# Trunk of a hybrid streaming encoder: memory tokens weighted ahead of the query scaling, two gate groups swapped, finer waits

## What is computed

```python
xn = rmsnorm(x, norm1_w)                     # 384 x 1024
proj = xn @ w_in                             # q,k,v | a,b | dn_gate | sc_b,sc_c,sc_h | mq | 3 gates of 1024
q,k,v = split(silu(causal_conv4(qkv)))       # width-4 causal convolution, 12 column groups of 128
q = l2norm(q) * 128**-0.5 ; k = l2norm(k)
o, state = gated_delta(q, k, v, g, beta)     # 64-frame blocks; sample sequences from a carried state
y_dn  = rmsnorm_head(o) * dn_norm_w * silu(dn_gate)        # 512 wide
y_sc  = sc_b * causal_conv3(sc_c * sc_h)                   # 256 wide
y_mem = attend(mq, rmsnorm(mem) @ w_mem_kv)                # 256 wide
merged = sig(g_dn) * (y_dn @ w_br[:512]) + sig(g_sc) * (y_sc @ w_br[512:768]) + sig(g_mem) * (y_mem @ w_br[768:])
h = x + merged @ w_o
y = rmsnorm(h + moe(rmsnorm(h)))             # 32 experts, top 4, 1024 x 1024 x 3 weights each
```

## Time and profile before

| what | value |
|---|---|
| median of the runs | 1447.47 us |
| the profiled execution's own time | 1438.7 us |
| its span, first to last instruction | 1436.8 us |
| PE busy | 1380.6 us (96%) |
| DVE busy | 404.1 us (28%) |
| ACT busy | 232.0 us (16%) |
| chain that ended last | PE 80%, DMA 14%, DVE 3%, ACT 2% |
| mean granted TensorE clock | 0.992 of full |

### The profile page before, as it was taken

How to read it: one execution, slowest core, us unless ns; L and a number is a source line. 1 busy time by engine, 2 the same in 40 slices (tenths; PEclk the granted TensorE clock), 3 DMA queues, 4 the chain that set the end, 5 groups by cost and what they waited for, 6 DMA issues and landing times.

```text
span 1436.8 us, 16371 instructions
## 1 busy us (share of the span) xinstructions
PE 1380.6 (96%) x7269; PEld 672.1 (47%) x7269; DVE 404.1 (28%) x751; ACT 232.0 (16%) x448; POOL 0.2 (0%) x4
## 2 busy tenths in 40 slices
PE   6999999989999899999999999999999999999996
PEld 4546677645554634434434344344343443434432
DVE  3565254261112431221221221212212122121223
ACT  3334231220001111111101111111011111111112
POOL 0000000000000000000000000000000000000000
PEclk9999999999999999999999999999999999999998
DMA  9343331012535589999999999999999999999993
GB/s 339 119 136 118 117 68 61 1 27 92 190 129 234 226 354 429 431 430 430 430 434 428 434 428 432 431 431 432 429 432 430 432 430 430 430 432 430 430 427 148
DMA packets 54072, 455.70 MB, mean 317 GB/s; under 512 B 12532, under 2 KB 21913, under 8 KB 39792
## 3 DMA queue, kind: packets, MB, share of 16 engines
q1 hardware_dynamic: 54000, 454.63, 76.5%
HBM read 449.98 MB, written 4.64 MB: 316 GB/s over the span
## 4 chain that ended last, share of the span: by engine, by line
PE 80%; DMA 14%; DVE 3%; ACT 2%; issue 1%; SPq 0%; DVEq 0%; ACTq 0%
PE ps L1075 38%; DMA sb_ring<-in_w_up_dram 13%; PE ps L752 8%; PE ps L561 7%; PE ps L1112 6%; PE ps L537 4%; PE ps L1051 3%; PE ps L968 3%; PE ps L766 3%; PE ps L601 1%; DVE sb_dg L1634 1%; DMA sb_ring<-in_w_br_dram 1%; PE ps L1012 1%; PE ps L847 1%; DMA sb_cst<-in_consts_dram 0%
## 5 line engine op out<-in xcount | busy, mean ns | idle before, releaser
L1075 PE MATMUL ps<-sb_ring,sb_xg 128*64 128x512 f32 x2048 | 455.6, 597 | 15.8 <-DMA sb_ring<-in_w_up_dram 11.9
L1075 PEld LDWEIGHTS ps<-sb_ring,sb_xg 128*64 128x64 f32 x2048 | 141.8, 137 | 282.9 <-issue 257.4
L1075 PE MATMUL ps<-sb_ring,sb_hidT 128*64 128x512 f32 x1024 | 226.1, 594 | 0.1
L1075 PEld LDWEIGHTS ps<-sb_ring,sb_hidT 128*64 128x64 f32 x1024 | 72.4, 137 | 139.9 <-issue 139.1
L1980 DVE TENSOR_TENSOR sb_hg<-ps,sb_biases 128x512 f32<-128x512 f32 x32 | 22.1, 691 | 404.1 <-PE ps L537 404.1
L752 PE MATMUL ps<-sb_xn,sb_ring 128*128 128x384 f32 x384 | 134.3, 495 | 0.0
L561 PE MATMUL ps<-sb_xn,sb_ring 128*128 128x384 f32 x384 | 126.3, 487 | 1.4 <-DVE sb_xn L1584 1.4
L2004 DVE TENSOR_TENSOR sb_h<-sb_h,ps 128x512 f32<-128x512 f32 x96 | 61.5, 683 | 133.8 <-PE ps L1112 124.0
L561 PEld LDWEIGHTS ps<-sb_xn,sb_ring 128*128 128x128 f32 x384 | 72.2, 190 | 50.8 <-DVE sb_xn L1584 1.8
L752 PEld LDWEIGHTS ps<-sb_xn,sb_ring 128*128 128x128 f32 x384 | 71.3, 191 | 48.6 <-issue 4.3
L1051 PEld LDWEIGHTS ps<-sb_onehot,sb_xn 128*128 128x128 f32 x720 | 81.5, 192 | 12.2 <-issue 12.2
(11 more groups left out here) (305 smaller groups left out, 945.3 us busy)
## 6 DMA issues: line engine op xcount, KB each, us to landing
sb_ring<-in_w_down_dram SPq DMA_DIRECT2D x28, 4096.0 KB, 26.5
sb_ring<-in_w_up_dram SPq DMA_DIRECT2D x27, 4096.0 KB, 29.3
sb_ring<-in_w_gate_dram SPq DMA_DIRECT2D x27, 4096.0 KB, 31.3
sb_ring<-in_w_in_dram SPq DMA_DIRECT2D x12, 2048.0 KB, 9.9
sb_ring<-in_w_gate_dram SPq DMA_DIRECT2D x10, 2048.0 KB, 10.9
sb_ring<-in_w_up_dram SPq DMA_DIRECT2D x10, 2048.0 KB, 14.4
sb_ring<-in_w_down_dram SPq DMA_DIRECT2D x8, 2048.0 KB, 12.6
sb_ring<-in_w_br_dram SPq DMA_DIRECT2D x2, 2048.0 KB, 8.3
```

Of the source, the lines that this page charges most:

```text
L1075: last = mm(o, x(k), columns(kind, w, i, j), start=(k == 0), stop=(k == KT8 - 1))
```

## The change

Four places are touched. The memory tokens' weighting and the last three convolutions stand ahead of the query scaling on VectorE, and TensorE's first memory product waits for one weighted tile and not for both. The sample output goes to words of its own (`o_tok`, in region r1), so that its copy out of PSUM no longer waits for the second output norm; that wait stands behind the transposes now. `output_norm(2, 4)` stands behind the last `mask` and ahead of the merges of that place. `group_unit` puts the gate columns of groups 16 and 17 ahead of both their branch products. The one wait for all 24 merges in front of w_o becomes a wait per block `mg[:, j]` inside the first 8 products.

```diff
--- before.py
+++ after.py
@@ -226,6 +226,7 @@
 
         nwk_s, qd_s = (r1[:, 1024 * k:1024 * k + 1024].rearrange("p (h s n) -> p h s n", h=HEADS, s=NSEQ) for k in range(2))
         oS, osq = t4(wk, 0), t4(wk, 1)
+        o_tok = t4(r1, 6)
         umask = [wk[:, 1024 + 512 * k:1536 + 512 * k].rearrange("p (s v) -> p s v", s=4) for k in range(2)]
 
         mg_at = nc.alloc_sbuf_tensor_at("sb_mg", [P, KT8 * TOK], F32, offset=slab_at + 4 * at["sp"])
@@ -251,6 +252,17 @@
 
         def group_start(k):
             return 10 * k if k <= SIDE else 10 * SIDE + 12 * (k - SIDE)
+
+        def group_unit(u):
+
+            k = next(k for k in range(GROUPS) if u < group_start(k + 1))
+            step = u - group_start(k)
+            if k not in (SIDE, SIDE + 1):
+                return k, step
+            step += 12 * (k - SIDE)
+            if step < 16:
+                return SIDE + step // 8, step % 8
+            return SIDE + (step - 16) // 4, 8 + step % 4
 
         def fill_bank(m):
             return 1 + m % 3
@@ -609,7 +621,7 @@
                     last = mm(bank(0)[32 * r:32 * r + 32, 0:TOK], wab[:, 4 * k + r, :], xnT[:, 4 * k + r, :], start=(k == 0), stop=(k == 1))
             last.then_inc(S["abp"], 1)
 
-            pe.wait_ge(S["xT"], 5)
+            pe.wait_ge(S["xT"], 4)
             weights_in(3)
             memory_columns(0)
             bank_free(PJ_WAB)
@@ -617,6 +629,7 @@
             for a in range(TILES):
                 last = mm(bank(pj_bank(PJ_WAB))[:, a * 8:(a + 1) * 8], ab4[:, a * P:(a + 1) * P], const("fold"), start=True, stop=True)
             last.then_inc(S["pj"], 1)
+            pe.wait_ge(S["xT"], 5)
             memory_columns(1)
             norm_sums(1)
             for a in range(2):
@@ -739,9 +752,8 @@
             def fill_to(units):
 
                 while filled[0] < units:
-                    k = next(k for k in range(GROUPS) if filled[0] < group_start(k + 1))
+                    k, step = group_unit(filled[0])
                     half, b, c = group(k)
-                    step = filled[0] - group_start(k)
                     n = GATE_PIECES[k // 4]
                     k0, kn, src = side[b]
                     if step < KT8:
@@ -939,7 +951,7 @@
             pe.wait_ge(S["otok"], 1)
             pe.wait_ge(S["onorm"], 1)
             for hh in range(HEADS):
-                last = tr(bank(4)[:, hh * P:(hh + 1) * P], osq[:, hh, :])
+                last = tr(bank(4)[:, hh * P:(hh + 1) * P], o_tok[:, hh, :])
             last.then_inc(S["otr"], 1)
             fill("ot", 0)
             output_sums(2, 4)
@@ -957,7 +969,6 @@
             fill_to(ALL_UNITS)
 
 
-            pe.wait_ge(S["mrg"], GROUPS)
             pe.wait_ge(S["st_upd"], 8)
             def mixed(a, half, j0=0, j1=KT8):
 
@@ -965,6 +976,8 @@
                 if a == 0:
                     weights_in(n)
                 for j in range(j0, j1):
+                    if a == 0 and half == 0:
+                        pe.wait_ge(S["mrg"], SIDE + j + 1)
                     last = mm(bank(2 * a + half), mg[:, j, a * P:(a + 1) * P], piece(TRUNK_SLOT[n])[:, j, :],
                               start=(j == 0), stop=(j == KT8 - 1))
                 if j1 == KT8:
@@ -1434,11 +1447,11 @@
             f(um[2], bank(0).rearrange("p (h n) -> p h n", h=4), ACT.Copy).then_inc(S["uev"], 1)
             sigmoids_of("us", 0)
             output_root(1)
-            act.wait_ge(S["yd"], 2)
             act.wait_ge(S["oready"], 1)
-            f(osq, bank(6).rearrange("p (h n) -> p h n", h=4), ACT.Copy).then_inc(S["otok"], 1)
+            f(o_tok, bank(6).rearrange("p (h n) -> p h n", h=4), ACT.Copy).then_inc(S["otok"], 1)
             sigmoids_of("os", 0)
             act.wait_ge(S["otr"], 1)
+            act.wait_ge(S["yd"], 2)
             output_parts(2, 4)
             sigmoids_of("ot", 0)
             output_root(2)
@@ -1647,18 +1660,17 @@
             for c in range(2, 8):
                 conv(c)
             norm_add(0)
-            conv(8)
-            norm_scale(0)
-            conv(9)
+            for c in range(8, 11):
+                conv(c)
             dve.wait_ge(S["vec_in"], 80)
             x_weighted(3)
             x_weighted(4)
-            conv(10)
             conv(11)
 
             v.tensor_copy(cov[:, :, 0:3], xp[:, :, LP - 3:LP])
             v.tensor_copy(cov[:, :, 3:27].rearrange("p c (s k) -> p c s k", k=3),
                           xp[:, :, LP:WP].rearrange("p c (s k) -> p c s k", k=3 + LS)[:, :, :, LS:LS + 3]).then_inc(S["co"], 1)
+            norm_scale(0)
 
             lgt = small[:, 64:88].rearrange("p (a k) -> p a k", a=3)
             az = small[:, 192:204].rearrange("p (a k) -> p a k", a=3)
@@ -1864,9 +1876,9 @@
                 last.then_inc(S["st_upd"], 1)
                 if hh + 2 < HEADS:
                     mask(hh + 2)
+                if hh == 1:
+                    output_norm(2, 4)
                 merges_of("sp", hh)
-                if hh == 0:
-                    output_norm(2, 4)
             dve.wait_ge(S["st_upd"], 8)
             v.tensor_copy(small[:, 211:212], states[:, 0, 0, 0:1]).then_inc(S["st_all"], 1)
             merges(ALL_UNITS)
```

## The result

| | before | changed |
|---|---|---|
| median of four runs | 1447.45 us (1447.4 to 1449.95) | 1427.99 us (1426.92 to 1430.54) |
| the profiled execution's own time, its span | 1438.7, 1436.8 us | 1430.54, 1428.7 us |
| its mean granted clock | 0.992 | 0.991 |

The ratio is 0.9873, 95% interval 0.9845 to 0.9902: 19.5 us faster, where 10.1 were forecast and the range went to 15.5. The two profiled executions lie only 8.1 us apart in span. A later set of six runs of the changed kernel gave a median of 1428.57, and one of the kernel before beside it 1445.02 (29 runs, 1438.19 to 1451.41); ratio 0.9893, interval 0.9858 to 0.9928.

A forecast was written before the change was run, and what follows sets the result against it. TensorE's waits in the trunk were taken as the bound, with the expert weight stream's start hanging on TensorE. 3.2 + 2.8 + 2.8 + 1.3 = 10.1 us off the 1447.47 median gave 1437.4 us; range 1432 to 1443.

The forecast's parts named there:

- Part 1: First memory product: with memory tokens weighted ahead of the query scaling, TensorE's whole wait goes, 3.2 us gained.
- Parts 2 and 3: End of the delta rule: sample output's own words and norm behind the last mask, together 2.8 us gained.
- both new waits: End of the delta rule: TensorE would wait about 1.2 us ahead of the sums and 1.0 us ahead of group 8.
- Part 4: Groups 16 and 17: two groups of gate columns cover the w_br load, 2.8 us gained.
- Part 5: Output projection: a finer wait at w_o hides the last merge behind seven products, 1.3 us gained.
- The pushed-back query scaling: VectorE, 11.5 us of reciprocal and product moved later: costs nothing, with a margin of 1.3 us before the softmax.
- the weight stream followed the trunk one for one: Expert stage: the stream's start hangs on TensorE's ring slot, so each us gained in the trunk counts once at the end.
- Rival (a): Clock at 260 to 280 and 500 to 510 us: moved stretches may spare or add 5.3 us, 1432 or 1442.7; chance 0.15.

The follow-up runs named there:

- wo_only_again: Second set of the kernel before with only the finer wait inside w_o's first products; twelve runs, mean 1443.5 us.
- control: The kernel before with no edit, run again; twelve executions, median 1445.43 us, ratio 1.0002.
- after_again: The changed kernel run again without a further edit; six runs, median 1428.57 us.
- denser: Changed kernel with three gate units for two in each gap of the state steps, five for three ahead of the sums; mean 1427.0 us.
- tokens_only: Kernel before with only the memory tokens ahead of the query scaling and the wait for one tile; mean 1439.6 us, ratio 0.9951.
- all_but_tokens: Changed kernel with the memory tokens as before; mean 1435.0 us, ratio 0.9938 to the kernel before.
- state_only: Kernel before with only the sample output's own words and the norm behind the last mask; mean 1442.5 us, ratio 0.9985.
- swap_only: Kernel before with only the gate columns of group 17 ahead of group 16's branch products; mean 1441.3 us, ratio 0.9976.
- kept_busy: Kernel before with idle products ahead of the first memory product, the output's transposes and the first delta branch product; mean 1440.2 us, ratio 0.9977.
- before_router_busy: Kernel before with idle products in the three short waits of the router's end; mean 1441.3 us, ratio 0.9974.
- router_busy: Changed kernel with idle products in the three short waits of the router's end; mean 1426.1 us.
- busy_at_tokens: Kernel before with four idle products only in the wait ahead of the first memory product; mean 1443.2 us, ratio 0.999.
- wo_router_busy: Kernel before with the finer wait at w_o and idle products in the router's end waits; mean 1442.2 us.

## Why the prediction was wrong

**Step by step, the working held.** Free of clock the changed kernel is 10.6 us under before, for a sum of 10.1. Part 1: 2.8 alone and 3.4 in the whole, for 3.2. Parts 2 and 3: 2.5 for 2.8, with both new waits in place and of their size. Part 4: 3.7 for 2.8; the load's landing varies, and the wait I took from one trace, 2.5 us, was at the small end of 2.5 to 3.1. That explains at most 0.6 of the 0.9 us; the rest is within the noise. Part 5: 1.1 for 1.3. The four parts alone add up to 10.1. The pushed-back query scaling cost nothing, and the weight stream followed the trunk one for one.

**The step that failed** is the one from the profiled execution to the median: "The median is 8.8 us above it, for which the trace gives no cause; the gains lie ahead of that stream, so I take them off the median unchanged". The cause was the granted clock. The profiled execution had kept its clock at all the waits that the change removes; other executions lose it at some of them, and with the waits these losses go: the changed kernel has 12.1 us of lost clock for 18.4, worth 5.6 us at the fitted slope. 10.6 + 5.6 = 16.2 us is the difference of the means, where 10.1 were forecast. The other 3.3 us of the measured 19.5 are the draw: all four runs of the kernel before stood at 1447.4 or above, where only a third of its 122 executions lie, and its mean is 1445.1. This second part is luck, and no step of the prediction could have given it. How far the traces account for the 6.3 us of lost clock can be estimated: the shares of traces that lose it at each removed wait, times what such traces lose there (3.7 us in the mean at the first memory product, 184 to 196 us counted in, and 1.7 at each of the others), add up to about 4. Where the rest goes is not located.

**Rival (a) had the mechanism and the wrong size and place.** It priced only the two stretches that this trace showed at the lower clock, 5.3 us, and called the effect even in sign, adding that the stalls at 88 and 304 us "did not cost the clock". In one execution they did not. In wo_only_again both did, and two further waits with them (the windows from 84, 304, 320 and 388 us above), and idle products in three of these waits gave back 4.9 us though no work was let in earlier. So the sign was not even: with the waits go the losses behind them. The prediction's own figures held the hint, a median 8.8 us over an execution with a mean clock of 0.992, which would have asked for a range down to 10.1 + 8.8 us under the median, 1428.6, although a part of the 8.8 us lies between 260 and 292 us, which the change leaves alone. The Trainium skill, "TensorE: Matmul & The Clock Gate", section "The HAM clock gate (the "warmup" mystery)", says that the chip's watch on TensorE's activity runs freely, and that one kernel therefore measured 6, 11 or 14 matmuls at the low clock at its start in different runs. The traces here agree in kind, in the middle of a kernel: the same 3.2 us wait ahead of the first memory product lost the clock in six of nine.

**Still open.** The loss between 260 and 292 us (about 3 us at the lower level in some traces, 17 in others) is the largest single loss in the traces that have it in full, and is in both kernels (17 us in control and in after_again), where TensorE is busy all the time, mostly with narrow products; `denser` did not settle whether wider work there helps. How the clock loss of the whole change divides between its four parts is not resolved: tokens_only had 3.1 us less lost clock and all_but_tokens, the other three together, 3.2 less, which would make two halves of the 6.3, but state_only and swap_only alone had none less, though the traces show losses at their waits too; with twelve runs a mean of lost clock is uncertain by 2 to 4 us.

## What to carry to other kernels

Before a gain is taken off a median, look how the executions spread and whether their time follows the mean clock; one trace shows one draw of it. A wait of TensorE of 2 to 3 us can cost twice, its own length and, in some executions, the products behind it at the lower clock, so removing it is worth more than its row says. Where a wait can't be removed, products that nobody reads can be put into it without overrunning it. Here they gave back 4.9, 3.8 and 2.8 us in kept_busy, before_router_busy and router_busy, and nothing clear of noise in busy_at_tokens and wo_router_busy.

## What was not expected of the hardware

The spread of one unchanged kernel on one core was 15 us of 1445 (1438.0 to 1453.2 in 122 executions), nearly all of it clock: 0.88 us of time per us of (1 - clock) x span. And the clock fell behind waits of 1.9 to 3.2 us in some executions and in others behind none of them: at 84 to 100 us the granted clock was 0.79 and 0.89 in the two traces shown, and full in the trace taken before. Behind one early wait of the same kind all five of 2.1 to 2.7 us lost the clock and none of the thirteen of 1.4 to 1.8 us did, yet a wait of 1.9 us further on lost it in three traces of ten and waits of 2.5 to 3.2 us kept it in others, so the length of the wait alone does not decide it.
